# Two-layer PEER step: sample rows multiplied from PSUM, a layer's attention in four PSUM banks, and searches cut into eight steps

## The reference, cut to what matters

```python
# dense part, for the prompt tile, then for the sample tiles
h = rms_norm(x, norm1_g) * (1 + sc1) + sh1
qa, ka, va, qb, kb, vb, ci, cb, cc = split_projection(h, w_in, ...)
oa = gqa_attention(qa, ka, va)            # 6 heads, one softmax each
ob = diff_attention(qb, kb, vb, lam)      # 6 heads, two softmax maps each
oc = short_conv_mixer(ci, cb, cc, conv_w, conv_b)
x  = x + g1 * merge_mixers(oa, ob, oc, ...)
# lookup part (peer_ffn), on h2 = the modulated rows
h2 = rms_norm(x, norm2_g) * (1 + sc2) + sh2
q  = (h2 @ wq).reshape(128, 8, 2, 128)
sc = einsum('thcd,hcnd->thcn', q, sub_keys)             # 8 heads, 2 halves, 128 keys
s1, i1 = top_k(sc[:, :, 0], 16); s2, i2 = top_k(sc[:, :, 1], 16)
top_s, pos = top_k(s1[..., None] + s2[..., None, :], 16)
eidx = ...                                              # 16 experts for each token and head
act  = gelu(einsum('thkd,td->thk', u_tab[eidx], h2))    # products with the rows of u
x    = x + g2 * einsum('thkd,...->td', softmax(top_s) * act * v_tab[eidx])
```

## Time and profile before

| | us |
|---|---|
| three runs, median (lowest to highest) | 3205.22 (3202.32 to 3216.55) |
| the profiled execution, own time | 3236.59 |
| its span in the trace | 3234.8 |
| DMA: 963.27 MB in the span | 298 GB/s on average |

### The profile page before, as it was taken

The page is one execution under the profiler, slowest core; times in us unless marked ns, Lnnn a source line. Parts: engine busy times, 40 slices in busy tenths (PEclk is TensorE's granted clock), DMA queues, the critical chain, the costliest instruction groups (busy, mean ns, idle before and its releaser), DMA issues.

```text
span 3234.8 us, 22432 instructions
## 1 busy us (share of the span) xinstructions
PE 1552.9 (48%) x6476; PEld 676.8 (21%) x6476; DVE 1635.3 (51%) x3970; ACT 278.2 (9%) x730; POOL 1715.8 (53%) x1601
## 2 busy tenths in 40 slices
PE   6666668567234433333445747856423222232334
PEld 2343235244001110111222225424300000000001
DVE  1406676454656555455532596543556555565420
ACT  0211013011000000010000103210100000000000
POOL 0004511355677777436665660247577777777755
PEclk9778765788557666666678875677765656665567
DMA  8668962589998999658999890379799999998988
GB/s 298 247 237 281 353 220 85 208 319 341 361 332 319 379 380 368 241 198 301 340 375 368 312 359 26 125 268 360 258 333 335 326 337 346 345 349 316 339 313 311
DMA packets 299017, 963.27 MB, mean 298 GB/s; under 512 B 28280, under 2 KB 30712, under 8 KB 298128
## 3 DMA queue, kind: packets, MB, share of 16 engines
q0 software_dynamic: 221184, 805.40, 67.9%
q1 hardware_dynamic: 77712, 156.44, 13.4%
HBM read 959.12 MB, written 2.62 MB: 297 GB/s over the span
## 4 chain that ended last, share of the span: by engine, by line
issue 24%; PE 22%; POOL 19%; DMA 18%; DVE 14%; another core or an unknown queue 1%; ACT 1%; POOLq 0%; SPq 0%; DVEq 0%; ACTq 0%
POOL ring L618 19%; DMA ring<-peer_v,v_rows 11%; PE ps_acc L875 7%; DVE ring L1381 4%; PE ps_mm L700 3%; PE ps_mm L754 2%; PE ps_mm L813 2%; DMA weights<-ada_w 2%; DMA ring<-peer_u,u_rows 2%; PE ps_mm L841 1%; PE ps_mb L780 1%; DMA weights<-w_in 1%; DMA weights<-peer_wq 1%; PE ps_tr L765 1%
## 5 line engine op out<-in xcount | busy, mean ns | idle before, releaser
L875 PE MATMUL ps_acc<-ring,coef_cols 128*32 128x512 f32 x3072 | 629.5, 959 | 1327.4 <-DMA ring<-peer_v,v_rows 1310.7
L1381 DVE CUSTOM_DVE_ANT_0 ring<-ring,h 128x1024 f32<-128x1024 f32 x768 | 917.2, 1224 | 636.2 <-DMA ring<-peer_u,u_rows 611.5
L618 POOL DMA_INDIRECT ring<-peer_u,u_rows x768 | 842.4, 1097 | 635.8 <-DVE dots L1381 386.3
L618 POOL DMA_INDIRECT ring<-peer_v,v_rows x768 | 839.4, 1093 | 398.0 <-issue 217.3
L875 PEld LDWEIGHTS ps_acc<-ring,coef_cols 128*32 128x32 f32 x3072 | 124.2, 148 | 1756.8 <-issue 1755.6
L700 PE MATMUL ps_mm<-weights,hT 128*128 128x512 f32 x480 | 217.3, 612 | 30.1 <-DMA weights<-w_in 25.6
L841 PE MATMUL ps_mm<-hT,weights 128*128 128x128 f32 (+1 forms) x1024 | 201.3, 355 | 26.5 <-DMA weights<-peer_wq 21.4
L841 PEld LDWEIGHTS ps_mm<-hT,weights 128*128 128x128 f32 x1024 | 171.7, 213 | 92.1 <-issue 53.0
L588 POOL TENSOR_SCALAR u_rows<-picks 128x16 uint32<-128x16 f32 x48 | 23.6, 493 | 302.7 <-DVE picks L1360 301.7
L700 PEld LDWEIGHTS ps_mm<-weights,hT 128*128 128x128 f32 x480 | 92.9, 196 | 154.6 <-issue 117.3
L1405 DVE TENSOR_TENSOR h<-h,ps_acc 128x1024 f32<-128x1024 f32 x6 | 7.3, 1222 | 197.7 <-PE ps_acc L875 197.7
(11 more groups left out here) (182 smaller groups left out, 1539.3 us busy)
## 6 DMA issues: line engine op xcount, KB each, us to landing
weights<-ada_w SPq DMA_DIRECT2D x24, 2048.0 KB
weights<-w_in SPq DMA_DIRECT2D x20, 2048.0 KB
weights<-peer_wq SPq DMA_DIRECT2D x16, 2048.0 KB
weights<-w_out SPq DMA_DIRECT2D x8, 2048.0 KB
ring<-peer_u,u_rows POOLq DMA_INDIRECT x768
ring<-peer_v,v_rows POOLq DMA_INDIRECT x768
weights<-peer_keys SPq DMA_DIRECT2D x4, 1024.0 KB
par<-params SPq DMA_DIRECT2D x2, 1026.0 KB, 7.0
```

Source lines behind the costliest of these rows:

```text
L618: pool.indirect_dma_start(ring[:, place % RING, :], None, src, bass.IndirectOffsetOnAxis(ap=rows, axis=0)).then_inc(row_full[place % RING] ...
L875: last = pe.matmul(ps_acc[QROWS * k:QROWS * (k + 1), b * NB:(b + 1) * NB], coef_cols[:, i // PART % 2, at:at + QROWS], ring[:, slot("v", n ...
L1381: dve.tensor_tensor_reduce(row, row, h2[:, n // (2 * UNIT) % T, :], 1.0, 0.0, ALU.mult, ALU.add, dots[:, n // UNIT % 2, n % UNIT:n % UNIT ...
```

## The change

The change has four parts.

1. **Dots of the sample tiles read their modulated rows from PSUM.** ACT copies `h2[:, tile]` into both banks of `ps_tr` before a sample tile's first dot (`hold_rows`, four copies in all), and the 512 dots of tiles 1, 2, 4 and 5 read `ps_tr` instead of `h2`. The prompt's 256 dots still read `h2`.
2. **Layer 1's prompt tile (`tight`) does without `ps_tr`,** since that pair is held by tile 2's rows meanwhile. Its transposes go to `ps_mm` and `ps_mb`; its scores have one buffer instead of two, and its transposed probabilities one instead of two.
3. **PE's order in that tile's attention:** the transposes of the head before come ahead of the next head's scores.
4. **A search is a generator with eight steps,** of which one runs at each of the places 8 to 15, 24 to 31, 40 to 47 and 56 to 63, each ahead of that place's dot. The searches that open a unit are still done in one piece.

```diff
+SAMPLES = [l * T + t for l in range(DEPTH) for t in S_TILES]
...
+        def tight(l, tiles):
+
+            return l > 0 and tiles == P_TILES
+
+        def transposed(l, tiles):
+            return ps_mm if tight(l, tiles) else ps_tr
+
+        def keys_at(l, tiles, j):
+            return ps_mb[:, NB:2 * NB] if tight(l, tiles) else tr(j)
+
+        def scores_at(l, tiles, g, n):
+            return mm(0, n) if tight(l, tiles) else mm(g, n)
+
+        def probs_at(l, tiles, head, n):
+            return mm(1, n) if tight(l, tiles) else tr(head, n)
+
+        def key_scores_at(l, tiles, i, n):
+            return ps_mb[:, (i % 2) * NB:(i % 2) * NB + n] if tight(l, tiles) else tr(i, n)
+
+        def conv_up(l, tiles):
+            return ps_mb[:, CW:2 * CW] if tight(l, tiles) else ps_mb[:, NB:NB + CW]
+
+        def buffers(l, tiles):
+
+            return 1 if tight(l, tiles) else 2
 
...
                 if l or tiles == S_TILES:
                     pe.wait_ge(ps_ready, group_nth(l, tiles, -1, 16))
+                if l and tiles == S_TILES:
+                    pe.wait_ge(u_used, l * 2 * T * UNIT)
                 yield from norm(l, tiles, 0)
                 pe.wait_ge(hT_ready, nth(l, tiles, 2, nt - 1))
...
                     for c in range(6):
                         col = QA + c * P if c < 3 else QB + (c - 3) * P
-                        last = pe.transpose(ps_tr[:, c * P:(c + 1) * P], proj[:, j, col:col + P], ident)
+                        last = pe.transpose(transposed(l, tiles)[:, c * P:(c + 1) * P], proj[:, j, col:col + P], ident)
                     last.then_inc(qT_mm, 1)
                     pe.wait_ge(qT_ready, nth(l, tiles, 1, j))
 
                     def scores(head):
                         for u in units(head):
                             g = j * UNITS + u
-                            if g >= 2:
-                                pe.wait_ge(exp_ready, nth(l, tiles, UNITS, g - 2))
+                            if g >= buffers(l, tiles):
+                                pe.wait_ge(exp_ready, nth(l, tiles, UNITS, g - buffers(l, tiles)))
                             m = u - A_HEADS
                             c, lo, n = (0, HD * (u // 3), HD) if u < A_HEADS else (1 + m // 4, DK * (m % 4), DK)
                             q = w_.qT[lo:lo + n, u % 3 if u < A_HEADS else 3 + m // 4, :]
                             k = w_.kT[lo:lo + n, c, :, :].rearrange("p j n -> p (j n)")
-                            pe.matmul(mm(g, nk * P), q, k, start=True, stop=True, tile_position=(lo, 0)).then_inc(score_mm, 1)
+                            pe.matmul(scores_at(l, tiles, g, nk * P), q, k, start=True, stop=True, tile_position=(lo, 0)).then_inc(score_mm, 1)
 
                     def transpose_probs(head):
...
-                        if head + 1 < HEADS:
+                        if head + 1 < HEADS and not tight(l, tiles):
                             scores(head + 1)
                         if head >= 1:
                             transpose_probs(head - 1)
+                        if head + 1 < HEADS and tight(l, tiles):
+                            scores(head + 1)
                         if head >= 2:
                             weigh_values(head - 2)
                         yield W_HEAD
...
+            def hold_rows(tau):
+
+                act.wait_ge(u_used, 2 * tau * UNIT)
+                act.wait_ge(ps_ready, group_nth(tau // T, S_TILES, 15, 16))
+                act.wait_ge(h_ready, nth(tau // T, S_TILES, 2, 2 * len(S_TILES) - 1))
+                act.activation(ps_tr[:], h2[:, tau % T, :], ACT.Copy).then_inc(h_held, 1)
 
             def copy_sum(unit):
                 act.wait_ge(v_used, (unit + 1) * UNIT)
@@ -1094,10 +1140,14 @@
                         spread(g.v, i // PART + 1)
                 if g.u is not None:
                     gelu_tanh(g.u)
+                    if g.u % 2 and not g.last and (g.u + 1) // 2 in SAMPLES:
+                        hold_rows((g.u + 1) // 2)
                 if g.v is not None and g.v % 2 == 0:
                     copy_sum(g.v)
                 if g.last:
                     side.end()
+                    if g.u is not None:
+                        hold_rows((g.u + 1) // 2)
...
                 dve.wait_ge(row_full[slot("u", n)], landed("u", n))
                 row = ring[:, slot("u", n), :]
-                dve.tensor_tensor_reduce(row, row, h2[:, n // (2 * UNIT) % T, :], 1.0, 0.0, ALU.mult, ALU.add,
+                tau = n // (2 * UNIT)
+                h = h2[:, 0, :]
+                if tau in SAMPLES:
+                    h = ps_tr[:]
+                    if n % (2 * UNIT) == 0:
+                        dve.wait_ge(h_held, held(tau))
+                dve.tensor_tensor_reduce(row, row, h, 1.0, 0.0, ALU.mult, ALU.add,
                                          dots[:, n // UNIT % 2, n % UNIT:n % UNIT + 1]).then_inc(u_used, 1)
 
             def coefficients(unit):
...
 
+                        for _ in routing:
+                            pass
                         while routed < g.u * UNIT_HEADS + AHEAD:
-                            route(routed)
+                            for _ in route(routed):
+                                pass
                             routed += 1
                     side.item()
                     if g.u is None:
@@ -1429,8 +1494,11 @@
                     head = g.u * UNIT_HEADS + i // TOPK + AHEAD
 
                     if i % TOPK == TOPK // 2 and head == routed and (head % P_HEADS or head // P_HEADS % T == 2):
-                        route(routed)
+                        for _ in routing:
+                            pass
+                        routing = route(routed)
                         routed += 1
+                    next(routing, None)
                     if i == GATE_AT:
                         gate_diffs(g.u)
                     if i == GATE_AT + 4:
```

51 lines of the change are left out of this document (30 added, 21 removed).

## The result

The changed kernel takes 3047.18 us (median of four runs, 3046.03 to 3062.32) where the kernel before takes 3203.77 us (median of four, 3199.70 to 3216.55): ratio 0.9514, 95% interval 0.9480 to 0.9548. Later, beside the control of another set of runs, the same kernel came to 0.9526 (0.9496 to 0.9556).

A forecast was written before the change was run, and what follows sets the result against it. POOL was taken as much the limit as the DMA engines in the lookup segments, the dense chain in the two long ones. Gains of 56 + 6 + 6 + 8 + 0 = 76 us took 3236.6 to 3160.6, median 3130 us; range 3060 to 3195.

The forecast's parts named there:

- What bounds the kernel: Lookup segments: POOL as much the limit as DMA, 540 of 597 us; gathers beside two-SBUF-operand dots take 1.99 us.
- together in the lookup segments: Five segments with lookups and no dense part: PSUM rows and stepped searches together gain 56 us, bounds 0 and 136.
- Searches in eight steps: Pieces of some 1.2 us fit DVE's wait for a row; no DVE time removed, lookup-segment gain priced jointly with PSUM dots.
- Units 1 and 7: Two spread searches each, in the attention, let PE and ACT go on: 8 us gained, bounds 0 and 39.
- Units 3 and 5: Segments of 210 and 225 us: 6 us gained, bounds 0 and 24.
- Units 0 and 6: Prompt units, dots still hold POOL, only searches spread: 6 us gained, bounds 0 and 19.
- Unit 4: Layer 1's prompt attention: 12 us lost to single-buffered scores, 12 us gained from a search no longer in a block; together 0.
- Copies to PSUM: ACT's four copies of 1023 ns each, behind a dense part or a tanh: taken as 0, at worst 5 us.
- the signs to look for: Sample gathers near 945 ns, units 0 and 6 above 1.1 us, units 8 to 10 at 185 to 190 us, POOL under 85%.
- the engines fill: Rival: queue never runs dry, lookup segments at 178 us, 116 + 42 us gained, median 3049 us; chance 0.12.
- Only the searches count: Rival: gathers stay at 1.11 us, only gaps behind searches go, 35 us gained, median 3170 us; chance 0.10.
- Slower: Rival: each of six differential heads in the prompt's attention costs 12 us, 70 in all, median 3240 us; chance 0.08.

The follow-up runs named there:

- the control: The changed kernel itself, unchanged, run again in another set against the kernel before: ratio 0.9526 (0.9496 to 0.9556).
- the memset run: Changed kernel plus a POOL memset of 96 columns, waited for, ahead of every gather: ratio 0.9918 (0.9896 to 0.9941) to the kernel before.
- the first traces: The profiled executions of the kernel before (3236.6 us) and of the changed kernel (3062.3 us).
- the second trace of before: The kernel before, no edit, traced once more: one execution, 3190.69 us.
- all blocks: Changed kernel with every search in one block again, PSUM rows and the prompt's four banks kept: ratio 0.9653 (0.9621 to 0.9685) to the kernel before.
- the four-bank run: Kernel before with only layer 1's prompt tile in four banks and PE's new order there: ratio 1.0007 (0.9984 to 1.0029).
- the set with slower transfers: A set of runs against the kernel before, which took 3270.41 us there; 64 v rows alone took 95 us at 366 GB/s.
- its near relative with steps in four units: Changed kernel with searches in eight steps only in units 0, 1, 6 and 7, elsewhere in one block: ratio 0.9779, repeated 0.9552, to the kernel before.

## Why the prediction was wrong

The direction was right, and so was the mechanism of the gathers; that of the searches was right in part; the size was half of what came. By its own steps:

- **What bounds the kernel.** POOL at nine tenths of the lookup segments, slow because a dot with both operands in SBUF holds a gather: right. That the second operand decides it is shown by the gathers (1120 and 1109 ns before, 959 and 938 with PSUM rows alone, 1172 and 1048 with steps alone); that POOL's time was the limit is shown by the memset run, which put it back and with it 45 us in units 8 to 10.
- **The step that failed** is the term "together in the lookup segments", 56 us with 1.45 us a gather as the floor. It measured 113 us between the first traces, and 982 - 888 = 94 us between the second trace of before and the control. The floor was read from one segment of v rows alone at a share of 0.97, in an execution with slower transfers; the same segment takes 85 us in the second trace of before, 1.33 us a gather. I had the rate at a share of 1.0 (386 GB/s, 174 us) as an outer bound only, and it is what came. With the limit named (POOL 540 of 597 us), the sum should have asked what the next limit allows once POOL falls to 1.23 us a gather, and that is the full DMA rate, 1.33 us a gather in the second trace of before. It asked instead how much of the present gap to a nearly full segment might close.
- **Searches in eight steps.** Priced with the PSUM rows in the lookup segments, they bring nothing there: 522 us in blocks, 527 and 525 in steps. The hole behind a search was closed by the PSUM rows. The 3 us of transfer time lost behind each search, which the prediction also gave the rival with the searches, was read behind one of the worst: the average over 18 is some 2.1 and 1.5 us in the two traces of before.
- **Units 1 and 7**, taken as 8 us (bounds 0 and 39): 12 + 8 = 20 us between the first traces; between all blocks and the control 16 + 8. Second trace of before to control: 10 + 9. The mechanism (PE and ACT go on beside the pieces) is shown for the last search of unit 0, which lies in the attention too and was not counted. The two searches of unit 1 itself come behind the attention; they cost through slots of the ring that came free late and v rows that PE then waited for, a path that the prediction did not have.
- **Units 3 and 5**, 6 us: 14 + 4 = 18 between the first traces, but 6 + 2 between the second trace of before and the control, so the term was about right and the rest the execution's. **Units 0 and 6**, 6 us: -1 + 2, and 2 + 7.
- **Unit 4.** The cost, 12 us: at most 5 by the segment, 0.0007 of the time by the ratio, with an interval of about 7 us to either side. What covers it: PE comes to the scores late (DVE's longest wait is 12.7 us, 13.5 in the second trace of before), and most of the exchanges behind it take DVE 0.2 to 1.4 us each. The waits of the change in that unit:

```profile
DVE rowmax L1281 <- PE ps_mm L791: 46.9, 12, 12.7
...
PE ps_mm L791 <- ACT scores L1013: 16.0, 12, 5.2
```

  The gain of the steps there, 12 us: 11 measured, and by the wait that was named. With the searches in blocks the same line reads:

```profile
PE ps_mm L791 <- ACT scores L1013: 22.1, 12, 12.7
```

- **v rows alone,** left at 0: 8 us between the first traces; the second trace of before has the 85 us too, so it is the execution's rate and not the change.
- **Copies to PSUM,** 0: 1016 ns each, no wait of DVE for them in the trace.

Of the signs to look for, the gathers, the prompt units, the DMA share, the dots and unit 4 came as written. The segments of units 8 to 10 took 176 us each, less than the 185 to 190 forecast, and so POOL's gathers and pauses did not fall under 85% of them but to 470 of 527 us, 89%.

Of the rivals, "the engines fill" was the one that came, at 3047 us for the 3049 forecast, its lookup segments at 178.6 us on average for the 178 forecast; it had 0.12, and the range ended at 3060. That it met the time to 2 us is partly luck: it had 116 + 42 us, and between the second trace of before and the control the parts are 94 + 52. "Only the searches count", which the first of the two sentences that the prediction takes from the Trainium skill (SBUF — State Buffer, Who interferes with whom) would have given, fell: the dots with one operand in PSUM hold no gather (952 and 941 ns), those with two do, in the same program (gathers in unit 6, a prompt unit, have a mean of 1.27 us). The section's other sentence, that two SBUF inputs block a GpSimd instruction that reads SBUF, agrees with both numbers. "Slower" fell with the four-bank run.

## What to carry to other kernels

When an engine's busy time plus its pauses fill nine tenths of a segment, work out which limit comes next once it is relieved, and take that as the likely result, not a part of the gap. Read that next limit where nothing else runs, in more than one execution: the transfer rate there was 366 GB/s in one set of runs and 394 in another. A DVE instruction that need not read two SBUF operands beside gathers that POOL issues should not: here that alone was worth 3.5%. Long blocks on one engine cost most beside a chain that passes through several. They held it up directly (8 us for one exponential) and through the ring (7 us for v rows ahead of a projection in PE's queue), and cost nothing beside gathers alone once the engine that issues them had time to spare.

## What was not expected of the hardware

The rate of the same gathers differed between executions and sets of runs: where POOL was not delayed and the dense weights were those of the change, 64 v rows alone took 85 or 86 us (391 to 395 GB/s) in eight traces, but 93 us in the first trace of before and 95 and 97 us in two of the set with slower transfers. What lay behind it no run here tells. At the slower rate the change is worth less: in the set where the kernel before took 3270 us, its near relative with steps in four units came to 0.9779, where beside the control it had 0.9552. A gather issued beside a dot with both operands in SBUF did not slow the dot: these dots have a mean of 1221 to 1225 ns in every trace, those on `ps_tr` 1218 to 1220; the wait falls on POOL, whose gathers in unit 6 have a mean of 1.27 us.
